# Gate arithmetic of the mLSTM spread over the batches of the sample attention, in one inference step of a hybrid decoder layer

## The reference, cut to what matters

```python
a = rms_norm(x, g_mix_pre);  z = a @ w_in            # mLSTM q,k,v,o; gates; attention q,k,v
# gates, per head and token: running maximum and running sum of the log forget gate
lf = log_sigmoid(f);  b = cumsum(lf)                  # b restarts in every chunk
m_t = max(m_{t-1} + lf_t, i_t)                        # stabiliser
w = exp(b_last - b + i - m_new);  decay = exp(b_last + m - m_new)
# sample attention: 8 new queries per sequence against 1024 cached keys + 8 new ones
s = q @ k_all.T * scale + bias;  p = softmax(s);  o = p @ v_all
mix = concat(h_mlstm, h_attention) @ w_out;  x = x + rms_norm(mix)
x = x + rms_norm((silu(hf @ w_gate) * (hf @ w_up)) @ w_down)
```

## Time and profile before

| what | value |
|---|---|
| median of three runs | 2991.03 us (2980.49 to 2997.17) |
| the profiled execution, its own time | 2981.75 us |
| its span, first to last instruction | 2979.8 us |
| PE busy / DVE / ACT / POOL, share of the span | 92% / 42% / 30% / 8% |
| mean granted TensorE clock | 0.968 of full |
| sample attention, from its first DMA issue to the gates stage | 474.1 to 593.7 us |
| gates stage | 593.7 to 634.0 us |
| mLSTM stage: first issue, first matmul | 634.0 us, 641.9 us |

### The profile page before, as it was taken

One profiled execution on the slowest core, in us unless ns is written; L12 is line 12 of the kernel. 1 busy time (PEld: TensorE's weight loads), 2 busy tenths in 40 slices (PEclk: granted clock), 3 DMA queues, 4 the chain that ended last, 5 costly groups with the idle time before them and its releaser, 6 DMA issues. The chain is left out here.

```text
span 2979.8 us, 48229 instructions
## 1 busy us (share of the span) xinstructions
PE 2751.4 (92%) x17582; PEld 1580.5 (53%) x17770; DVE 1241.7 (42%) x3050; ACT 884.2 (30%) x2196; POOL 233.7 (8%) x620
## 2 busy tenths in 40 slices
PE   7998886849999999969979999999999999999998
PEld 6666765527585766835534444444444444444443
DVE  6336775356656566557722222221121211122144
ACT  6116885334343444423322101220011210022111
POOL 2001221101121121211100000000000000000000
PEclk9999999969999999979989999999999999999999
DMA  5123345420211011044321022101321103310034
GB/s 189 72 68 69 94 99 160 123 61 9 58 30 31 30 31 52 2 141 149 128 83 43 14 105 62 42 21 71 134 76 38 42 28 134 113 43 21 35 143 177
DMA packets 172554, 224.96 MB, mean 75 GB/s; under 512 B 13297, under 2 KB 138052, under 8 KB 171740
## 3 DMA queue, kind: packets, MB, share of 16 engines
q1 hardware_dynamic: 167734, 210.16, 22.3%
q0 software_dynamic: 4656, 12.65, 1.4%
HBM read 156.85 MB, written 65.92 MB: 75 GB/s over the span
## 5 line engine op out<-in xcount | busy, mean ns | idle before, releaser
L2513 DVE TENSOR_TENSOR f_hidden<-f_silu,f_ps_up 128x512 f32<-128x512 f32 (+1 forms) x110 | 65.2, 592 | 627.0 <-ACT f_silu L2454 627.0
L114 PE MATMUL f_ps_gate<-act_lo,f_w_hi 128*128 128x512 bf16 (+1 forms) x858 | 277.2, 342 | 15.8 <-DVE f_w_lo L2500 8.5
L114 PE MATMUL f_ps_y<-f_down_lo,f_h_hi 128*128 128x512 bf16 (+1 forms) x727 | 276.2, 380 | 9.4 <-issue 7.0
L115 PE MATMUL f_ps_up<-act_hi,f_w_lo 128*128 128x512 bf16 (+1 forms) x880 | 284.5, 342 | 0.0
L114 PE MATMUL f_ps_up<-act_lo,f_w_hi 128*128 128x512 bf16 (+1 forms) x880 | 284.5, 342 | 0.0
L113 PE MATMUL f_ps_up<-act_hi,f_w_hi 128*128 128x512 bf16 (+1 forms) x880 | 284.5, 342 | 0.0
L113 PE MATMUL f_ps_y<-f_down_hi,f_h_hi 128*128 128x512 bf16 (+1 forms) x744 | 282.8, 380 | 0.5
L115 PE MATMUL f_ps_y<-f_down_hi,f_h_lo 128*128 128x512 bf16 (+1 forms) x738 | 280.3, 380 | 1.1
L115 PE MATMUL f_ps_gate<-act_hi,f_w_lo 128*128 128x512 bf16 (+1 forms) x858 | 277.2, 342 | 1.2
L113 PE MATMUL f_ps_gate<-act_hi,f_w_hi 128*128 128x512 bf16 (+1 forms) x836 | 268.8, 341 | 1.2
L2454 ACT ACTIVATE f_silu<-f_ps_gate 128x512 f32<-128x512 f32 (+1 forms) x110 | 57.1, 519 | 655.0 <-PE f_ps_up L115 655.0
(11 more groups left out here) (397 smaller groups left out, 5448.1 us busy)
## 6 DMA issues: line engine op xcount, KB each, us to landing
y_part_rows<-f_total SPq DMA_DIRECT2D x48, 512.0 KB, 2.6
f_total<-y_part_rows SPq DMA_DIRECT2D x48, 512.0 KB, 3.6
f_raw_gate<-in_w_gate SPq DMA_DIRECT2D x22, 512.0 KB, 5.1
f_raw_up<-in_w_up SPq DMA_DIRECT2D x22, 512.0 KB, 6.2
f_raw_down<-in_w_down SPq DMA_DIRECT2D x22, 512.0 KB, 3.4
m_w_raw<-in_w_in SPq DMA_DIRECT2D x20, 512.0 KB, 6.7
o_comb<-pattern_rows SPq DMA_DIRECT2D x16, 594.0 KB, 5.7
nx<-in_x_prompt SPq DMA_DIRECT2D x16, 512.0 KB, 3.3
```

Of the source, the lines that this page charges most:

```text
L114: pe.matmul(out, w_hi, x_lo, start=False, stop=False)
L115: return pe.matmul(out, w_lo, x_hi, start=False, stop=last)
L2513: nc.vector.tensor_tensor(hidden[u][:, 0:n], act_out[u][:, 0:n], ps_up[u][:, 0:n], ALU.mult).then_inc(hidden_done, 1)
```

## The change

The gates stage is dissolved into the sample stage, which becomes `stage_sample_and_gates`:

- **Early keys.** The keys of batch 0 and the bias are loaded from SP's list in the first step of prompt attention's last sequence. To have room, the q weights share their tile with these keys, and `vb` and the penalties share one with the first mLSTM weights.
- **Queues.** POOL issues no DMA any more. SP issues keys, values, the gates' small tables, and after the values of the last batch the first mLSTM weights (`m_w_raw0`); the mLSTM stage leaves that load out, and still loads its constants first.
- **Order at the start.** Scores of batch 0 before the keys of batch 1 are turned. ACT: keys 0, the three passes of |f|, exp, ln, exponential of batch 0, keys 1. DVE: copy of the forget gate, batch 0, small tables, keys 1, `lf`.
- **Gates in the batches.** DVE, behind its work of a batch: 0 the running maximum, 1 the running sum and the eight short maxima, 2 chunk ends and two passes, 3 and 4 the logs of the weights. ACT, behind its work of batches 3, 4, 5: one exponential pass each. PE: after the values of batch 6 the decays and three groups of `stack`, in batch 7 the two others.
- **Values stationary.** The values (128 columns) become the stationary operand and the probabilities (16 columns) the moving one. The result lands turned in `ps_o`; the 16 result rows (L993) and their turning (L963) go.

The passes on the gates have the sizes that they had; each now waits for its own semaphore instead of one common counter. The diff, cut to its core (the functions that compute the gates on DVE are those of L1201 to L1253 under names of their own):

```diff
+def cached_rows(queue, g, tile, loaded, b, first):
+
+    cols = slice(first, first + D_A)
+    far = g.cache_kv[ds(b, 1), 0:FAR, cols].rearrange("o (f n r) c -> (o f) n r c", f=FAR_TILES, r=FAR_STRIDE)
+    for f in range(FAR_TILES):
+        queue.dma_start(tile[:, f, :], far[f, :, 0:DEC_SEQ, :]).then_inc(loaded, 16)
+    near = g.cache_kv[ds(b, 1), FAR:, cols].rearrange("o (t p) c -> p (o t) c", p=P)
+    queue.dma_start(tile[:, FAR_TILES:CACHE_TILES, :], near).then_inc(loaded, 16)
+
...
-        w_q_hi, w_q_lo = sb("a_w_q_hi", [P, KT, D_A], BF16), sb("a_w_q_lo", [P, KT, D_A], BF16)
+        w_q_hi, w_q_lo = g.a_w_q[:, 0, :, :], g.a_w_q[:, 1, :, :]
...
-            vb = [sb(f"a_vb{i}", [P, PAIRS, 2, 2, HD_A + 1], BF16, rows_scope) for i in range(2)]
+            vb = [g.a_vb[:, i * PAIRS * VROW:(i + 1) * PAIRS * VROW].rearrange("p (q i a c) -> p q i a c", q=PAIRS, i=2, a=2)
+                  for i in range(2)]
...
-        bias = [sb(f"a_bias{i}", [P, 2, 2 * P]) for i in range(2)]
+        bias = [g.m_w_raw0[:, i * 4:(i + 1) * 4, :].rearrange("p (h a) c -> p h (a c)", h=2) for i in range(2)]
...
                     k = sequence_of(2 * step)
+                    if k == len(sequence_end) - 1 and 2 * step == sequence_end[k - 1]:
+                        sp.wait_ge(q_ready, PAIRS * n_q)
+                        cached_rows(sp, g, g.s_k_raw0, g.s_k_in0, 0, 0)
+                        sp.dma_start(g.s_bias, g.sample_bias).then_inc(g.s_bias_in, 16)
                     if 1 <= k < len(sequence_end) - 1:
...
+        TOK_BANKS = [ps_big[0], ps_big[1], ps_small[1], ps_big[0], ps_big[1]]
+        groups = [list(range(t, t + 4)) for t in range(0, TILES, 4)] + [[TILES]]
+        EARLY_GROUPS = 3
...
-                load(sp, k_raw, k_in, 1, 1, 0)
+                def keys(b):
+                    cached_rows(sp, g, k_raw[b % 2], k_in[b % 2], b, 0)
+
+                def values(b):
+                    cached_rows(sp, g, v[b % 2], v_in[b % 2], b, D_A)
+                    sp.dma_start(v[b % 2][0:DEC_SEQ, CACHE_TILES, :], g.kv_sample[ds(b * DEC_SEQ, DEC_SEQ), D_A:])\
+                        .then_inc(v_in[b % 2], 16)
+
+                keys(1)
+                conv_src = g.w_conv.rearrange("i (c p) -> i c p", p=P)
+                for i in range(CONV_W):
+                    sp.dma_start(conv_rows[i * 2 * H_M:(i + 1) * 2 * H_M, :], conv_src[i, :, :]).then_inc(tab_in, 16)
+                sp.dma_start(gain_rows, g.g_mh).then_inc(tab_in, 16)
+                sp.dma_start(hist_rows, g.state_conv).then_inc(tab_in, 16)
+                sp.dma_start(n_rows, g.state_n).then_inc(tab_in, 16)
+                values(0)
+                with nc.allow_non_contiguous_dma(reason="a transposed state of 40 numbers"):
+                    sp.dma_start(m_state[:, :], g.state_m.rearrange("b h -> h b")).then_inc(carries_in, 16)
+                sp.dma_start(b_sum[:, :], g.carries).then_inc(carries_in, 16)
+                sp.dma_start(own[:, :, :], g.own_head).then_inc(carries_in, 16)
+                sp.wait_ge(k_turned, PAIRS)
+                keys(2)
+                values(1)
+                sp.wait_ge(k_turned, 2 * PAIRS)
+                keys(3)
                 for b in range(2, DEC_BATCH):
-                    sp.wait_ge(k_turned, (b - 1) * PAIRS)
-                    load(sp, k_raw, k_in, b, b % 2, 0)
+                    if b + 2 < DEC_BATCH:
+                        sp.wait_ge(k_turned, (b + 1) * PAIRS)
+                        keys(b + 2)
+                    sp.wait_ge(o_ready, b - 1)
+                    values(b)
+                sp.dma_start(g.m_w_raw0[:, :, :], g.w_in[:, COL_Q:COL_Q + P].rearrange("(k p) c -> p k c", p=P))\
+                    .then_inc(g.m_w_in0, 16)
+                sp.wait_ge(ends_done, 4)
+                with nc.allow_non_contiguous_dma(reason="45 numbers"):
+                    sp.dma_start(g.m_prompt.rearrange("o h -> h o"), m_end[:, TILES - 1:TILES]).then_inc(out_dma, 16)
+                    sp.dma_start(g.m_sample.rearrange("b h -> h b"), m_end[:, TILES:]).then_inc(out_dma, 16)
+                sp.wait_ge(u_done, 1)
+                sp.dma_start(g.u_dram, u[:, :]).then_inc(out_dma, 16)
                 sp.wait_ge(o_hi, 2 * PAIRS)
                 sp.wait_ge(o_lo, 2 * PAIRS)
                 for part in range(2):
                     sp.dma_start(g.mix_a_dram[part], mix_a[part][:, :]).then_inc(mix_out, 16)
                 sp.wait_ge(mix_out, 2 * 16)
+                sp.wait_ge(out_dma, 3 * 16)
...
+                nc.gpsimd.memset(stack[:, :], 0.0).then_inc(zeroed, 1)
+                nc.gpsimd.memset(tab[:, :, TILES * TAB_SIZE:TAB_DECAY], 0.0).then_inc(zeroed, 1)
+                nc.gpsimd.memset(ones[:, :], 1.0).then_inc(zeroed, 1)
...
+                def turn_tables():
+                    pe.wait_ge(tab_in, 7 * 16)
+                    n = CONV_W * 2 * H_M
+                    nc.tensor.transpose(ps_o[:, 0:n], conv_rows, g.ident[0:n, 0:n])
+                    nc.tensor.transpose(ps_o[:, 64:64 + H_M], gain_rows, g.ident[0:H_M, 0:H_M])
...
-                    hold(o_kept, b)
+                    hold(p_kept, b)
...
+                    if b == DEC_BATCH - 1:
+                        for i in range(EARLY_GROUPS, len(groups)):
+                            turn_tokens(i)
...
+                    if b == 0:
+                        pe.wait_ge(tables_done, 1)
...
+                        out = slice(b * HT + pair * 2 * DEC_SEQ, b * HT + (pair + 1) * 2 * DEC_SEQ)
...
-                            mm = nc.tensor.matmul(ps_p[0:2 * DEC_SEQ, cols], p_t[slot][0:n, own], v[slot][0:n, tile, cols], start=(tile == 0),
+                            mm = nc.tensor.matmul(ps_o[:, out], v[slot][0:n, tile, cols], p_t[slot][0:n, own_heads], start=(tile == 0),
...
+                    if b == DEC_BATCH - 2:
+                        spread_decays()
+                        for i in range(EARLY_GROUPS):
+                            turn_tokens(i)
+
+                for pair in range(PAIRS):
+                    turn_k(0, 0, 0, pair)
                 scores(0, 0)
+                turn_tables()
+                for pair in range(PAIRS):
+                    turn_k(1, 1, 0, pair)
                 batches(attend)
-                pe.wait_ge(o_kept, DEC_BATCH)
-                for i in range(DEC_BATCH * PAIRS):
...
+                def soften():
+
+                    nc.scalar.activation(soft[:, :], gates[F_GATE_ROW:, :], ACT.Abs).then_inc(soft_done, 1)
+                    act.wait_ge(soft_done, 1)
+                    nc.scalar.activation(soft[:, :], soft[:, :], ACT.Exp, scale=-1.0).then_inc(soft_done, 1)
+                    act.wait_ge(soft_done, 2)
+                    nc.scalar.activation(soft[:, :], soft[:, :], ACT.Ln, bias=1.0).then_inc(soft_done, 1)
...
-                    act.wait_ge(o_ready, b + 1)
-                    nc.scalar.activation(o_rows[:, ds(b * D_A, D_A)], ps_p[0:2 * DEC_SEQ, 0:D_A], ACT.Copy).then_inc(o_kept, 1)
+                    if b == 3:
+                        act.wait_ge(decay_log, 1)
+                        nc.scalar.activation(decay[:, :], decay[:, :], ACT.Exp).then_inc(decay_exp, 1)
+                        act.wait_ge(m_done, 1 + DEC_BATCH)
+                        token_row(ROW_M, m)
+                    if b == 4:
+                        act.wait_ge(log_w_done, 1)
+                        token_row(ROW_W, log_w[:, :])
+                    if b == 5:
+                        act.wait_ge(log_e_done, 1)
+                        token_row(ROW_E, log_e[:, :])
 
                 keep_k(0, 0)
+                soften()
+                exponential(0, 0)
                 keep_k(1, 1)
-                exponential(0, 0)
                 batches(attend)
 
-                act.wait_ge(o_done, 1)
+                act.wait_ge(o_ready, DEC_BATCH)
...
                         prepare(b + 2, slot)
-
-                dve.wait_ge(bias_in, 16)
+                        prepare_new(b + 2, slot)
+                    if b == 0:
+                        running_maximum()
+                    if b == 1:
+                        running_sum()
+                        sample_maxima()
+                    if b == 2:
+                        segment_ends()
+                        log_inputs()
+                    if b == 3:
+                        dve.wait_ge(log_u_done, 1)
+                        log_weights(stack[0:H_M, :], shift, log_w, log_w_done)
+                    if b == 4:
+                        own_decays()
+                        dve.wait_ge(u_done, 1)
+                        log_weights(u, m_in, log_e, log_e_done)
+
+                nc.vector.tensor_copy(fgate[:, :], gates[F_GATE_ROW:, :]).then_inc(f_copied, 1)
+                dve.wait_ge(g.s_bias_in, 16)
+                prepare_new(0, 0)
                 prepare(0, 0)
-                prepare(1, 1)
                 mask_scores(0, 0)
                 normalise(0, 0)
+                keep_tables()
+                prepare_new(1, 1)
```

(46 more changed lines are left out.)

329 lines of the change are left out of this document (133 added, 196 removed).

## The result

The changed kernel takes 2967.97 us (median of 12 runs, 2958.88 to 2974.73), the kernel before 2985.59 us in the same comparison (12 runs): a ratio of 0.9937, 95% interval 0.9924 to 0.9949, or 17.6 us less. The forecast was 39.1 us less. The direction holds, but less than half of the gain is there, and 2967.97 lies 1 us above the widest range that the prediction gives (2927 to 2967).

What follows compares the result with a forecast made beforehand. TensorE is busy 92% of the span, so time can be won only where it stands still; 2.1 + 1.6 + 2.7 + 0 - 2.8 - 39.2 - 3.5 = -39.1 us, forecast 2948 us, range 2932 to 2964, with rivals 2927 to 2967.

Steps and rivals of the forecast that it cites:

- the second rival: VectorE's gate passes in the sample batches don't hide but add up in full: +21.8, 2970 us; chance 0.08.
- The start: Start of the sample stage: loop scores +2.1 us later despite early keys, and +1.6 us for scores at 1.2 GHz.
- The passes: VectorE's gate passes in the batches: mostly hidden in waits of 3.41 and 1.51 us, batches 1 and 2 overrun, +2.7 us.
- The swapped product: Value product in the sample batches: 42 records at 0.12 us, 5.0 us, the small gain mostly hidden: 0.
- the first rival: Short moving operand pays: value products at 0.077 us a record take 3.2 us, -10.8, 2937 us; chance 0.12.
- the end: From the last scores to ScalarE's first split: 17.5 us instead of 20.36, -2.8 us.
- The third rival: TensorE stays at 1.2 GHz through the sample stage because of gaps the passes open: +81, 3029 us; chance 0.02.
- The gates stage: Stage between sample attention and mLSTM goes: 40.2 us less about 1 us for clearing semaphores, -39.2 us.
- The mLSTM weights: Start of mLSTM stage: weights are there, VectorE waits for three constants; first matmul -3.5 us, not 5.5.
- The fourth rival: Early loads don't come through: first keys late or holding up prompt attention, at most +8, 2956 us; chance 0.03.
- the prediction's last part: Signs of being wrong: value products near 3.2 us, batches of 15 us and more, clock 0.5 beyond 503 us, TensorE waiting for keys or values.

Runs made afterwards that it cites:

- e1b: Same kernel as e1, run again beside later experiments: 2951.55 us, ratio 0.9891.
- e1: Changed kernel with the value product as before (probabilities stationary, 128 moving columns; result rows kept by ScalarE, turned one batch later): 2953.21 us, ratio 0.9885.
- e7: e1 with one more scan of 4.41 us, result unused, on VectorE behind batches 3 and 4 each: 2956.28 us, ratio 0.989.
- e2: Kernel before with the swapped product alone (values stationary, 16 moving columns), nothing else of the change: 3009.33 us, ratio 1.0078.
- e8: e5 with VectorE's wait for the mLSTM stage's three constants moved behind its first split of weights: 2946.26 us, ratio 0.9866.
- e4: Changed kernel with one more bf16 matmul of 16 moving columns behind each of the product's 18 full tiles a batch: 2982.74 us (one run).
- e5: e1 with the copy of the forget gate moved behind the first batch's low parts: 2948.44 us, ratio 0.987.
- e10: e8 with the first keys and the bias loaded at the start of the sample stage again: 2952.58 us, ratio 0.9879.

## Why the prediction was right, and where it was wrong

By its own steps, all in us, with the stage cut at the loop's first scores, the last scores, ScalarE's first split and the next stage's first issue:

| stretch | forecast | changed kernel | e1b |
|---|---|---|---|
| first issue to the loop's first scores | 23.4 | 23.6 | 22.4 |
| to the last scores (six batches) | 77.5 | 93.4 | 77.6 |
| to ScalarE's first split | 17.5 | 26.5 | 19.3 |
| to the mLSTM stage's first issue | 5.5 | 5.6 | 5.6 |
| to its first product | 4.4 | 4.4 | 4.4 |
| sum | 128.3 | 153.4 | 129.4 |

The number of the prediction came near for a reason that it doesn't have. Its range reaches up to 2967 for passes that don't hide (the second rival), which e1 and e7 refute; what filled that room was the clock, to which it gave 0.02. The good agreement of e1b with the forecast, 77.6 and 77.5 over six batches, is partly luck too: the passes cost less than forecast, but the result rows that e1 turns in each batch, which the changed kernel doesn't have, cost 0.28 us a batch (530.40 to 530.68), 1.7 in all.

```profile
530.40 0.35 PE L1012 MATMUL s_ps_o<-ident,s_o_rows 16*128 16x16 f32 x3
530.68 0.61 PE L1038 MATMUL s_ps_p<-ident,s_probs 48*128 48x48 f32 x7
```

- **The start** (+2.1 and +1.6): right. The scores began at 499.27, and the whole stage 1.6 us late, which leaves 497.7 for a forecast 497.5. The low clock there came as foreseen: the first batch of the loop takes 14.43 in e1b against 12.49 in its last, 1.9 for a forecast 1.6; in e1 it is 2.5.
- **The passes** (+2.7): mechanism right, too large. e1b pays 0.44 and 0.33 (12.92 and 12.81 us against 12.48). In the loop the eight short maxima take 1.16 us, not the 2.02 of the earlier trace rows, the short copies of batch 2 take 0.89, not 1.19, and the cover is 5.2 to 5.3 us, not 4.92.
- **The swapped product** (0): this step failed, and it is nearly all of the error. The price of a record was right, 0.126 for a forecast 0.12, and so the first rival (0.077 a record) fell. But "0" priced the records at the clock that the loop had before, and took it that the clock would stay. e1, which differs from the changed kernel in the product alone, shows that it costs 153.4 - 130.3 = 23.1 us of stage (130.3 is the mean of e1 and e1b), e2 shows 20.9 by another way. Both prices are net of the result rows and their turning, which go with the swap. The table shows where they fall: 15.8 in the loop (93.4 against 77.6) and 7.1 at the end, where the changed kernel takes 9.0 more than forecast.
- **The third rival**, TensorE at 1.2 GHz through the stage, had the right effect, with a chance of 0.02. Its cause, gaps, is refuted by e1 and by the 20.00 of 20 us for which TensorE is busy at 0.59. The prediction asked only what would make TensorE idle, not what it would be doing while busy. Its size, 81 us, took every record at half speed; from 500 to 600 us the clock is 0.72 on average, and part of what the records lose falls into waits (the 0.94 us at a batch's start is gone at 516.57 and 533.89).
- **The gates stage** (-39.2): right, 5.6 us stay from the first split to the next stage for a forecast 5.5.
- **The mLSTM weights** (-3.5): right to the tenth for the first product, with its reason: VectorE waits 2.65 us for `m_member`, and e8 takes that wait away. The sum stops at that product, though, and the second part of the weights is only 1.0 us earlier than before (ScalarE splits it from 641.59 before, 7.6 us behind the stage's first issue, and from 631.28, 6.6 behind, in the changed kernel). At ScalarE's first pass on a result 2.8 us are left (15.3 and 12.5 us behind the issue). The fourth rival, early loads that don't come through, fell: TensorE turns the first keys at the stage's first issue.
- **The time of a weight load.** The prediction had said of the Trainium skill (TensorE: Matmul & The Clock Gate, LDWEIGHTS) that the trace agrees that 128 stationary columns make the swap dear. At 128 columns it does: weight loads of 1.73 us for 14. But the Trainium skill gives there a load time in proportion to the columns, and e1b's loads of 16 columns take 1.20 us for 12, so 0.100 each against 0.124; there the trace disagrees.
- **The fall of the clock.** The same page of the Trainium skill (HAM oscillation — how this bites in real kernels) puts the repeated fall of the clock down to waits that leave TensorE idle. Here it fell in stretches without any wait.

What the prediction's last part named as signs of being wrong is what came: "a clock of 0.5 beyond 503 us" (0.59 on average from 500 to 520 us, 0.61 from 520 to 540) and "batches of 15 us and more" (17.30, 17.32 and 16.43 us for three of the six in the loop). The first mLSTM matmul, forecast at about 603 us, came at 629.1.

## What to carry to other kernels

Price a change of a matmul's form twice: the record, and the clock of everything around it. A product that mostly loads weights and streams few columns can let TensorE's clock fall although it never waits, and then its neighbours pay; here a swap with the same 0.12 us a record cost 21 to 23 us, while arithmetic of another kind, 40 us of it, hid almost free in the waits of VectorE. Count that cover as the waits between dependent steps, not as idle time in all, and change forms one at a time, since the gain of one part (the gates) covered the loss of the other.

## What the runs showed that was not expected

- TensorE's granted clock fell while it was busy without a break: 0.59 and 0.61 in two stretches of 20 us with 20.00 us busy each, and e4 likewise (0.67).
- More work made the kernel faster: with 144 more matmuls of 128 columns the stage takes 143.5 us for 153.4, and the total is 2960.53 us for 2967.97 (one run against a median).
- The copy of the forget gate takes VectorE 2.93 us at the start of the stage, while POOL's memsets run, and 1.25 us in e5, after them. First the rows of the changed kernel, then that of e5:

```profile
475.68 1.86 POOL L956 MEMSET g_stack<- 128x2112 f32 x1 [8.26 <-POOLq L425]
475.72 2.93 DVE L1275 COPY g_lf<-gates 5x2112 f32<-5x2112 f32 x1 [4.70 <-PEq L425]
```

```profile
487.41 1.25 DVE L1292 COPY g_lf<-gates 5x2112 f32<-5x2112 f32 x1
```

  In e5 the first instruction of VectorE in the stage, now a small cast, is held instead: it takes 1.85 us beside a memset of 1.86 us, where the same cast takes 0.17 in the loop.

```profile
480.81 1.86 POOL L957 MEMSET g_stack<- 128x2112 f32 x1 [8.46 <-POOLq L425]
480.84 1.85 DVE L1162 CAST s_k_hi<-k_new 128x24 bf16<-128x24 f32 x1 [4.90 <-PEq L425]
```

  No run moved POOL's memsets alone, so that they are the cause is likely and not shown.
- The sample stage's first issue differs by 12 us between executions (472.99 in e10, 485.02 in e1), more than most of the steps weighed here.
